# Operands of the scan's preparation in PSUM, and 128x128 block-diagonal keys in the scan's levels

## What is computed

```python
wt = jnp.tanh(wl)
for d in range(2):
    w_log = -jax.nn.softplus(-(p['rwkv_w0'][d] + wt @ p['rwkv_w2'][d])) - 0.5
    decay = jnp.exp(-jnp.exp(w_log))
    a = jax.nn.sigmoid(p['rwkv_a0'][d] + al @ p['rwkv_a2'][d])
    kk = heads(k * p['rwkv_k_k'][d]);  kk = kk / max(norm(kk), 1e-12)
    kd = heads(k * (1.0 + (a - 1.0) * p['rwkv_k_a'][d]))
    dirs.append((decay, kd, -kk, kk * heads(a)))
...
def step(S, inp):                      # one token of the scan
    r_t, w_t, k_t, v_t, a_t, b_t = inp
    sa = jnp.einsum('bhij,bhj->bhi', S, a_t)
    S = S * w_t[:, :, None, :] + sa[..., :, None] * b_t[:, :, None, :] + v_t[..., :, None] * k_t[:, :, None, :]
    return S, jnp.einsum('bhij,bhj->bhi', S, r_t)
```

## Time and profile before

| | us |
|---|---|
| median of three runs | 2294.09 |
| lowest and highest | 2288.39, 2295.02 |
| time of the profiled execution | 2289.43 |
| its span, first to last instruction | 2287.4 |
| TensorE busy in it | 2162.4 |
| VectorE, ScalarE, GpSimd busy | 958.9, 663.2, 872.0 |
| preparation of the scan, first layer, about | 434 to 497.8 |
| its three visits | 497.8 to about 620 |

### The profile page before, as it was taken

How to read it: one execution, slowest core, us unless ns; L and a number is a source line. 1 busy time by engine, 2 the same in 40 slices (tenths; PEclk the granted TensorE clock), 3 DMA queues, 4 the chain that set the end, 5 groups by cost and what they waited for, 6 DMA issues and landing times.

```text
span 2287.4 us, 44913 instructions
## 1 busy us (share of the span) xinstructions
PE 2162.4 (95%) x19484; PEld 1780.5 (78%) x19484; DVE 958.9 (42%) x1411; ACT 663.2 (29%) x1178; POOL 872.0 (38%) x602
## 2 busy tenths in 40 slices
PE   6999899989899999999999999989989989999997
PEld 3888477668778888888888778857759867888886
DVE  2002355386743723315142520335476645452452
ACT  3110366632412211102011320146652323221221
POOL 3333333172144224333242542235253144454454
PEclk9999999999997999999999899999999988999999
DMA  7311200210131112222123331120120042333231
GB/s 281 100 52 54 74 2 1 98 38 4 39 130 46 56 56 65 65 65 65 56 74 127 113 112 56 38 74 2 62 74 4 13 158 64 92 101 101 83 111 55
DMA packets 45463, 163.73 MB, mean 72 GB/s; under 512 B 5504, under 2 KB 5504, under 8 KB 45024
## 3 DMA queue, kind: packets, MB, share of 16 engines
q1 hardware_dynamic: 44480, 158.29, 21.2%
q0 software_dynamic: 800, 2.69, 0.4%
HBM read 158.86 MB, written 2.10 MB: 70 GB/s over the span
## 4 chain that ended last, share of the span: by engine, by line
PE 85%; DVE 6%; ACT 4%; issue 3%; POOL 1%; DMA 1%; SPq 0%; DVEq 0%; ACTq 0%; POOLq 0%
PE ps L1567 80%; PE ps L1893 3%; ACT flat L872 1%; DMA flat<-wmod_dram 1%; PE ps L2180 0%; DVE flat L1362 0%; DVE part_h L1436 0%; POOL flat L703 0%; DVE flat L1371 0%; DVE flat L1180 0%; DVE flat L1351 0%; POOL flat L614 0%; ACT hT L886 0%; POOL wparts L568 0%; DVE flat L1416 0%
## 5 line engine op out<-in xcount | busy, mean ns | idle before, releaser
L1567 PE MATMUL ps<-part_hi,wparts 128*128 128x512 f32 (+1 forms) x2640 | 701.9, 352 | 10.1 <-POOL wparts L568 5.9
L1567 PEld LDWEIGHTS ps<-part_hi,wparts 128*128 128x128 f32 x2640 | 468.0, 190 | 82.7 <-DVE part_h L1436 5.5
L1567 PE MATMUL ps<-part_h,wparts 128*128 128x512 f32 (+1 forms) x1320 | 462.9, 351 | 0.0
L1567 PE MATMUL ps<-flat 64*64 64x32 f32 (+8 forms) x8200 | 420.8, 257 | 29.9 <-DVE flat L1371 14.5
L1567 PEld LDWEIGHTS ps<-flat 64*64 64x64 f32 (+4 forms) x8200 | 322.0, 141 | 117.9 <-issue 92.1
L606 POOL TENSOR_TENSOR wparts<-flat,wparts 128x1024 fp32r<-128x1024 f32 x96 | 241.0, 2511 | 411.0 <-ACT wparts L1081 409.6
L1567 PE MATMUL ps<-part_mlp,wparts 128*128 128x512 f32 (+1 forms) x1152 | 309.9, 354 | 0.6 <-issue 0.6
L1567 PEld LDWEIGHTS ps<-part_h,wparts 128*128 128x128 f32 x1320 | 250.9, 190 | 33.8 <-issue 1.7
L1567 PEld LDWEIGHTS ps<-part_mlp,wparts 128*128 128x128 f32 x1152 | 204.9, 189 | 31.3 <-issue 0.7
L1567 PE MATMUL ps<-part_lo,wparts 128*128 128x512 f32 (+1 forms) x576 | 204.0, 354 | 0.0
L1558 DVE TENSOR_TENSOR flat<-flat,ps 128x768 f32<-128x768 f32 (+1 forms) x64 | 52.5, 820 | 355.7 <-PE ps L1567 355.7
(11 more groups left out here) (224 smaller groups left out, 2825.7 us busy)
## 6 DMA issues: line engine op xcount, KB each, us to landing
flat<-w_dram SPq DMA_DIRECT2D x128, 512.0 KB, 3.6
flat<-wmod_dram SPq DMA_DIRECT2D x88, 512.0 KB, 5.9
flat<-win_dram SPq DMA_DIRECT2D x40, 512.0 KB, 3.6
flat<-wout_dram SPq DMA_DIRECT2D x16, 512.0 KB, 3.6
hT<-wmod_dram SPq DMA_DIRECT2D x8, 512.0 KB, 7.7
xT<-xT_dram SPq DMA_DIRECT2D x8, 384.0 KB, 6.4
flat<-rope_dram SPq DMA_DIRECT2D x2, 1024.0 KB, 6.5
out_dram<-xT SPq DMA_DIRECT2D x8, 256.0 KB, 2.1
```

Source lines behind the costliest of these rows:

```text
L1567: return pe.matmul(out, lhsT, rhs, start=start, stop=stop)
```

## The change

Two things are done.

1. *Preparation.* ScalarE leaves kd's factor and the decay's sigmoid in the bank that it read, and puts `ei` into two areas of PSUM by turns (`ps[2048:]` for even n, `ps[1024:]` for odd n); VectorE reads them there. As the banks are now held longer, waits and order move: TensorE makes all four key spreads after tile 3, its tiles 4 to 7 wait for VectorE's kd, its tiles 8 and 9 and the gate for the scans; VectorE takes nkk and kd in the order 0, 1, 0, 1, 2, 3, 2, 3; ScalarE's `ei` 1 waits for the last scan, and 2 and 3 for VectorE's kd products; both kd products of direction 0 stand among the bh; two rows of the modulation use bank 7 instead of bank 4, and the second gate tile the same bank as the first. The first visit pairs x = 1 only after all of kd.
2. *Levels.* VectorE's mask of the keys is three passes: two write the blocks of c = 0 and c = 1 on the diagonal of 128x128 arrays (`DIAG`), the third the rest in `ABR`, in a denser layout. ScalarE writes zeros to the arrays once a layer. TensorE forms X in 8 products of 128x128 by 128x32 in place of the 16.

```diff
--- before.py
+++ after.py
...
         HALF = [F_WORK + W_SCAN + x * SCAN_HALF for x in range(2)]
-        ei = wv(W_RN, 4, TOK)
+
+        def ei(n):
+
+            at = 1024 if n % 2 else 2048
+            return ps[:, at:at + TOK]
+
+        AT_NKK, AT_KEYED = (1, 2, 5, 6), (3, 4, 7, 8)
+        DIAG = ((HALF[0] + 512, F_WORK + W_SCAN + 2 * SCAN_HALF), (RING + 5 * 256, HALF[1] + 512))
 
         FOUR = ((0, 0), (1, 1), (0, 1), (1, 0))
...
@@ -941,11 +948,11 @@
                         ins = nc_.activation(aa[:, n - 2, :], ps[:, o:o + TOK], ACT.Sigmoid, bias=par(l, "a0", n - 2))
                         ins.then_inc(s_rpe, 1)
                         act.wait_ge(s_rpe, 12 * l + n + 1)
...
                     else:
-                        ins = nc_.activation(sg[:, n - 6, :], ps[:, o:o + TOK], ACT.Sigmoid, bias=par(l, "w0", n - 6))
+                        ins = nc_.activation(ps[:, o:o + TOK], ps[:, o:o + TOK], ACT.Sigmoid, bias=par(l, "w0", n - 6))
...
                                    scale=-DECAY).then_inc(s_dec, 1)
-                    nc_.activation(ei[:, n, :], cs[n], ACT.Exp, scale=DECAY).then_inc(s_ex, 1)
+                    if n == 0:
+                        act.wait_ge(s_kkn, 8 * l + AT_NKK[3])
+                    elif n == 1:
+                        act.wait_ge(s_cs, 4 * (l + 1))
+                    else:
+                        act.wait_ge(s_prep, 5 * l + n - 1)
+                    nc_.activation(ei(n), cs[n], ACT.Exp, scale=DECAY).then_inc(s_ex, 1)
                     act.wait_ge(s_dec, 4 * l + n + 1)
...
                 act.wait_ge(s_rp, 12 * l + 12)
-                nc_.activation(gtok[:, 4:6, :], ps[:, 1024:1536].rearrange("p (b f) -> p b f", b=2), ACT.Copy).then_inc(s_rpe, 1)
+                nc_.activation(gtok[:, 4:6, :], ps[:, 0:512].rearrange("p (b f) -> p b f", b=2), ACT.Copy).then_inc(s_rpe, 1)
+                act.wait_ge(s_modps, 5 * l + 4)
+                act.wait_ge(s_side, 7 * l + 4)
+                act.wait_ge(s_prep, 5 * l + 4)
+                for x, g in ((0, 0), (1, 0), (1, 1), (0, 1)):
+                    ins = nc_.activation(cells(-1, DIAG[x][g], [1, 512]), km[:, M_AB:M_AB + 1].to_broadcast([P, 512]), ACT.Copy)
+                ins.then_inc(s_gate, 1)
...
 
-                for n in range(4):
-                    dve.wait_ge(s_ksp, 4 * l + n + 1)
-                    o = 2048 + (n % 2) * 1024
-                    V.scalar_tensor_tensor(out=nkk[:, n, :], in0=zv[:, R_K + n % 2, :], scalar=omm[:, 26 + n:27 + n], in1=ps[:, o:o + TOK],
-                                           op0=ALU.mult, op1=ALU.mult).then_inc(s_kkn, 1)
-
-                for n in range(4):
-                    dve.wait_ge(s_aa, 4 * l + n + 1)
-                    V.tensor_tensor(kd[:, n, :], kd[:, n, :], zv[:, R_K + n % 2, :], ALU.mult).then_inc(s_kkn, 1)
+                for n in (0, 1, 4, 5, 2, 3, 6, 7):
+                    k, o = n % 4, (n % 2) * 1024
+                    if n < 4:
+                        dve.wait_ge(s_ksp, 4 * l + n + 1)
+                        V.scalar_tensor_tensor(out=nkk[:, n, :], in0=zv[:, R_K + n % 2, :], scalar=omm[:, 26 + n:27 + n],
+                                               in1=ps[:, 2048 + o:2048 + o + TOK], op0=ALU.mult, op1=ALU.mult).then_inc(s_kkn, 1)
+                    else:
+                        dve.wait_ge(s_aa, 4 * l + k + 1)
+                        V.tensor_tensor(kd[:, k, :], ps[:, o:o + TOK], zv[:, R_K + n % 2, :], ALU.mult).then_inc(s_kkn, 1)
...
                 for n in range(4):
@@ -1349,29 +1368,28 @@
                         dve.wait_ge(s_rp, 12 * l + 10)
                     at, step = (0, 1) if n < 2 else (TOK - 1, -1)
                     V.tensor_tensor_scan(cells(-1, CS[n] * TOK + at, [step, TOK]), smask,
-                                         cells(-1, F_WORK + W_SG + n * TOK + at, [step, TOK]), 0.0,
+                                         bank(-1, (n % 2) * 1024 + at, [step, TOK]), 0.0,
                                          ALU.mult, ALU.add).then_inc(s_cs, 1)
 
...
 
-                    return V.tensor_tensor(x[:, n, :], x[:, n, :], ei[:, n, :], ALU.mult)
+                    return V.tensor_tensor(x[:, n, :], x[:, n, :], ei(n), ALU.mult)
...
-                    V.scalar_tensor_tensor(out=bh[:, n, :], in0=bh[:, n, :], scalar=-1.0, in1=ei[:, n, :],
+                    V.scalar_tensor_tensor(out=bh[:, n, :], in0=bh[:, n, :], scalar=-1.0, in1=ei(n),
                                            op0=ALU.mult, op1=ALU.mult)
-                    if n == 0:
-                        dve.wait_ge(s_side, 7 * l + 5)
-                        times(kd, 0)
+                    if n < 2:
+                        dve.wait_ge(s_side, 7 * l + 5 + n)
+                        times(kd, n).then_inc(s_prep, 1)
...
                 ins.then_inc(s_prep, 1)
-                dve.wait_ge(s_side, 7 * l + 6)
-                for n in range(1, 4):
+                for n in range(2, 4):
                     ins = times(kd, n)
                 ins.then_inc(s_prep, 1)
...
                             bass.AP(km, M_PAIR, [[NKM, P], [64, 2], [0, 4], C1]), ALU.mult))
-                        V.tensor_tensor(cells(-1, h + ABR, [256, 4], [1, 256]), bank(-1, o, [256, 4], [1, 256]),
-                                        km[:, M_AB:M_AB + 256].unsqueeze(1).to_broadcast([P, 4, 256]),
+                        if s == 0:
+                            dve.wait_ge(s_gate, 3 * l + 2)
+                        for c in range(2):
+                            V.tensor_tensor(cells(c, DIAG[x][0] + 64 * c, [DIAG[x][1] - DIAG[x][0], 2], [P, 4], C1),
+                                            bank(c, o, [P, 2], [256, 4], C1),
+                                            bass.AP(km, 64 * c * NKM + M_AB, [[NKM, 64], [P, 2], [0, 4], C1]), ALU.mult)
+                        V.tensor_tensor(cells(-1, h + ABR, [P, 4], [64, 2], C1), bank(-1, o + 64, [256, 4], [P, 2], C1),
+                                        bass.AP(km, M_AB + 64, [[NKM, P], [0, 4], [P, 2], C1]),
                                         ALU.mult).then_inc(s_abm[x], 1)
...
-                    pe.wait_ge(s_rpe, 12 * l + n - 1)
+                    if n == 10:
+                        pe.wait_ge(s_cs, 4 * l + 3)
+                    else:
+                        pe.wait_ge(s_rpe, 12 * l + 11)
                     for b in range(first, last):
-                        c = (n % 2) * 1024 + (b - first) * 256
+                        c = (b - first) * 256
                         mm(ps[:, c:c + 256], zv[:, R_GL, b * P:(b + 1) * P], g2a, True, False)
                         ins = mm(ps[:, c:c + 256], zv[0:32, R_MISC, b * P:(b + 1) * P], g2b, False, True)
...
                     if m >= 2:
-                        pe.wait_ge(s_kkn, 8 * l + m - 1)
+                        pe.wait_ge(s_kkn, 8 * l + AT_NKK[m - 2])
...
                     if n == 8:
-                        pe.wait_ge(s_kkn, 8 * l + 3)
-                        ring_row(4)
-                    if n >= 2:
+                        pe.wait_ge(s_kkn, 8 * l + AT_NKK[3])
+                        ring_row(7)
+                    if n in (2, 3):
                         pe.wait_ge(s_rpe, 12 * l + n - 1)
+                    elif 4 <= n < 8:
+                        pe.wait_ge(s_kkn, 8 * l + AT_KEYED[n - 4])
+                    elif n >= 8:
+                        pe.wait_ge(s_cs, 4 * l + n - 7)
...
                     if n == 3:
                         pe.wait_ge(s_krec, l + 1)
-                        spread_keys(0)
-                        spread_keys(1)
-                    if n == 5:
-                        spread_keys(2)
-                        spread_keys(3)
+                        for m in range(4):
+                            spread_keys(m)
...
-                pe.wait_ge(s_kkn, 8 * l + 4)
+                pe.wait_ge(s_kkn, 8 * l + AT_NKK[3])
                 pe.wait_ge(s_modrow, MOD_FROM[l] + 5)
                 mod_columns(scan_rows, 3, COL_SCAN)
-                ring_row(4)
+                ring_row(7)
                 gate(11, 4, 6)
...
-                pe.wait_ge(s_prep, 3 * l + 1)
+                pe.wait_ge(s_prep, 5 * l + 3)
...
                     if s == 0:
-                        for x in range(2):
-                            paired(s, x)
-                        pe.wait_ge(s_prep, 3 * l + 2)
+                        paired(s, 0)
+                        pe.wait_ge(s_prep, 5 * l + 4)
                         pe.wait_ge(s_modc, 3 * l + 2)
+                        paired(s, 1)
...
@@ -2096,14 +2124,13 @@
                             for g in range(2):
                                 for p in range(2):
                                     for f in range(2):
-                                        for c in range(2):
-                                            ins = mm(bank(c, o + g * P + (2 * p + f) * 32, [1, 32]),
-                                                     cells(c, h + ABR + p * 512 + f * 256 + g * P, C1),
```

(36 more changed lines are left out.)

## The result

The changed kernel takes 2474.36 us (2472.93 to 2475.9 in 4 runs) against 2293.19: a ratio of 1.0795, interval 1.0777 to 1.0813. The direction was forecast, the size was not: +181 us, where the forecast had +48 (2342 from a median of 2294.09), and far outside its range of 2323 to 2366.

A forecast was written before the change was run, and what follows sets the result against it. Preparation was taken as bound by VectorE, then GpSimd; levels by TensorE. 47.4 + 6.6 + 5.6 - 10 = +49.6 us gave 2339 from the profiled execution, 2344 from the median; forecast 2342, range 2323 to 2366.

The forecast's parts named there:

- Part 1: X in the levels: 160 products of 128x128 at 110 ns, 7.9 us more a visit, +47 us in six.
- rivals on the fast side: X's price: per instruction, 30.3 ns, 2263 us, chance 0.07; or a 128x128 load as the pair, 60 ns, 2292, chance 0.05.
- the strided one: Rival on X: strided 32 columns cost as much as the bonus's strided 128, 141 ns, giving 2369 us; chance 0.06.
- Part 2: Levels: TensorE's changes between 64x64 and 128x128 cost 0.22 us a round trip, 30 round trips, +6.6 us.
- Part 3: VectorE's key mask: three passes for one delay TensorE 1.4 us in visits two and three of each layer, +5.6 us.
- Part 4: Preparation: fewer VectorE and GpSimd collisions, first X about 5 us earlier a layer, -10 us for both.
- the 128x128 pitch near 110 ns: Sign in the levels: 960 matmuls of 128x128 with 32 columns, at a pitch near 110 ns.
- The level pieces: Sign: unbroken TensorE stretches of the levels, each some 9 us longer than the 22 to 25 of before.

The follow-up runs named there:

- 128-column form: Changed kernel with each X product streaming its 32 columns four times over (128 columns), same 128x128 weights: 2361.96 us, ratio 1.0298 to the kernel before.
- diagonal form: Changed kernel with X as 16 64x64 products from the diagonal blocks: 2317.1 us; with the second ring row earlier and unread products filling waits, 2323.73.
- With the clock held: Changed kernel with X's 32 columns streamed four times, second ring row ahead of the modulation columns, and unread products in three TensorE waits: 2352.82 us, ratio 1.0266.
- reordered and with fillers: Change's preparation with levels as before, second ring row ahead of three modulation columns, unread 256-column products in three TensorE waits: 2279.09 us, ratio 0.9940.

## Why the prediction was wrong in size

**The step that failed is in Part 1**: "no 128x128 matmul with 32 columns is in the trace, so I bound it by neighbours with the clock at 1.00". The price of 110 ns was right (112 at the upper clock). Multiplying it by 960, with T left at 30.3 ns, assumed that the new stream keeps the upper clock. It doesn't: 213 ns for X and 52 for T at 0.50, and the kernel is 112 us slower than its 128-column form. Neither the sum, the range nor any rival held that case. The measured 112 ns does rule out the rivals on the fast side, and the strided one. (The rule cited there from the Trainium skill, TensorEngine Tiling (Array Packing), section Instruction Overhead, is not borne out: 32 columns with 128x128 weights cost 112 ns, with 64x64 weights 30.)

The warning stood in the trace of before, in rows that the prediction didn't use, 719.8 to 735 us, where 73 products with 128x128 weights stream one column each:

```profile
719.80 15.10 PE L1567 MATMUL ps<-kf,flat 128*128 128x1 f32 x73
```

```profile
724.00:728.00 4.00, 4.00 (x21) 4.00 (x20) 0.00 (x0) 0.87 (x2) 3.84 (x4) 0.50 0.02 4
728.00:732.00 4.00, 4.00 (x21) 4.00 (x20) 0.00 (x0) 0.00 (x0) 3.92 (x3) 0.50 0.59 158
```

TensorE is full and the clock is 0.50. The prediction took its price from the same kind of stream in a stretch of 2 us that still had 1.00, and saw the clock fall only where TensorE stood half idle. Levels with two thirds of their time in such instructions lie between these rows and the levels of before, and needed a rival: both prices doubled, for all or part of the visits. Such a rival can be priced from these rows (an estimate): the 17.6 + 9.7 us of X and T in a visit, once more, is up to 164 us in six.

**Part 2** (0.22 us a round trip): 0.19 with 128 columns; right in size.

**Part 3** (1.4 us in four visits): the mechanism was right, the size not. Three visits waited 1.65 to 1.67 us, the fourth 4.16, and the first visits had 1.2 us each that the forecast put in its preparation: about 11 us instead of 5.6. It was also priced as if a wait cost only its length; the diagonal form lost some 36 us of clock as well.

**Part 4** (-10 us): the mechanism was right. Scans took 1.7 us and GpSimd's products 5.16. What failed is the sentence "The last ring row, gate 11 and its two ScalarE copies end near 480.6, before the first pairing needs them": GpSimd writes into the buffer that the ring row is the last to read, and could start only at 479.37, where the forecast had 476.7. With that row earlier and the waits filled the first X came 5.4 us earlier in layer one and 6.9 in layer two, and the kernel took 14 us less than before. As changed, the preparation alone gave nothing measurable (2291.69 against 2292.58): its first X came no earlier (67.95 and 68.31 us after the tanh), and in layer two 20 us of the levels ran near 0.5.

**With the clock held** the change costs 2352.82 - 2290.39 = 62 us, inside the forecast's range but more than its 49.6. X takes 9.4 us a visit more instead of 7.9 (56 in six instead of 47), T's 0.7 makes 4, the masks 11 instead of 5.6, and the preparation, reordered and with fillers, gave 14 (ratio 0.9940) instead of 10. These add up to 57 of the 62.

**What was foreseen of the signs**: the 128x128 pitch near 110 ns was there in 274 of 930 pairs, in the stretches at 1.00. The level pieces, forecast some 9 us longer, were 9.4 longer with 128 columns (34.76 against 25.37) and 26.7 as changed.

## What to carry to other kernels

When an edit makes fewer and larger weight loads with a short moving side, cost it at both levels of the granted clock, and for all that runs beside it: find the rows in which a full TensorE streams few columns, and read their clock. If the weights set the pace anyway, wider streams are free and can pay (128 columns instead of 32 were 112 us faster here). A wait of one or two microseconds ahead of such a stream can be followed by ten or twenty at the lower clock; filling it with unread products cost nothing here where it lay under another engine's work (0.9994 on the kernel before).

## What the runs showed of the hardware

- A TensorE that was busy 100% of the time had a granted clock of 0.50 in levels with 128x128 weights and 32 columns, in levels with 64x64 weights and 16 columns, and with 128x128 weights and one column. 64x64 with 32 columns kept 1.00 where it had it, and in several visits, not in all, stayed low for 12 to 20 us where it came out of a wait. 128x128 with 128 kept 1.00 nearly throughout (mean of the execution 0.970 to 0.978), with 64 mostly (0.967).
- The cost of an fp32 product with little to stream is that of its weights: 112 ns from start to start for 128x128 with 32, 64 and 128 columns alike; 29 ns for 64x64 in two corners with 16 columns and 30 with 32. At the lower clock 213 for 128x128 with 32 columns, and 52 for 64x64 with 32.
- Repeating the moving columns two or four times with a step of zero added nothing to the 112 ns.
- A change between 64x64 and 128x128 products and back cost 0.19 us.
